# Packed value columns, a shared root and an early copy of the first head in the second attention of a two-layer block

## The reference

```python
h = rms_norm(x, norm_g)
mq, mk, mv, mg, dq, dk, dv, dg = split(h @ w_in)      # 8 standard heads of 64; 4 differential heads
# standard heads: causal softmax attention with a linear bias by distance
m_out = softmax(mq @ mk.T * scale - slope * dist) @ mv * silu(mg)
# differential heads: two softmaxes over one value of width 128, then a norm of its own
d_out = (softmax(q1 k1) - lam * softmax(q2 k2)) @ dv
d_out = rms_norm(d_out, subln) * 0.8 * silu(dg)
x = x + concatenate([m_out, d_out]) @ w_out
```

## Time and profile before

| | us |
|---|---|
| median of 3 runs | 1016.03 (1015.81 to 1016.11) |
| the profiled execution, its time | 1016.16 |
| its span | 1014.0 |
| TensorE busy | 1002.1 (99%) |
| VectorE busy | 557.6 (55%) |
| GpSimd busy | 502.3 (50%) |
| ScalarE busy | 454.1 (45%) |

### The profile page before, as it was taken

How to read it: one execution, slowest core, us unless ns; L and a number is a source line. 1 busy time by engine, 2 the same in 40 slices (tenths; PEclk the granted TensorE clock), 3 DMA queues, 4 the chain that set the end, 5 groups by cost and what they waited for, 6 DMA issues and landing times.

```text
span 1014.0 us, 13704 instructions
## 1 busy us (share of the span) xinstructions
PE 1002.1 (99%) x5051; PEld 835.4 (82%) x5051; DVE 557.6 (55%) x943; ACT 454.1 (45%) x682; POOL 502.3 (50%) x296
## 2 busy tenths in 40 slices
PE   9999999999999999999999999999999999999998
PEld 7888888888888988888888888889888778777787
DVE  6799897887633964334334310116715276676731
ACT  7222346898644532322322322233454347667630
POOL 4444365842346134444444465453387545755562
PEclk9999999999999999999999999999999999999999
DMA  7232222212244032332322323333132120111112
GB/s 258 83 104 93 95 83 67 80 63 84 73 176 151 17 102 86 103 101 85 103 100 87 103 104 104 104 123 106 43 104 83 63 84 22 64 63 43 42 63 83
DMA packets 26402, 91.11 MB, mean 90 GB/s; under 512 B 3056, under 2 KB 3184, under 8 KB 26224
## 3 DMA queue, kind: packets, MB, share of 16 engines
q1 hardware_dynamic: 26352, 90.42, 26.4%
HBM read 88.31 MB, written 2.10 MB: 89 GB/s over the span
## 4 chain that ended last, share of the span: by engine, by line
PE 89%; DVE 7%; ACT 2%; issue 1%; DMA 1%; POOL 0%; SPq 0%; DVEq 0%
PE ps L463 27%; PE ps L465 27%; PE ps L464 27%; PE ps L927 2%; PE ps L951 1%; DVE resid L2014 1%; PE ps L624 1%; PE ps L640 1%; DVE a_lo L1664 1%; DMA resid<-x_t 1%; DVE sq_x L1657 1%; DVE q_raw L1657 1%; DVE mix L1657 1%; DVE b_lo L1664 1%; PE ps L656 0%
## 5 line engine op out<-in xcount | busy, mean ns | idle before, releaser
L2362 POOL TENSOR_TENSOR w_lo<-w_raw,w_hi 128x1024 fp32r<-128x1024 f32 x137 | 325.8, 2379 | 410.6 <-ACT w_hi L1128 357.9
L1128 ACT ACTIVATE w_hi<-w_raw 128x1024 fp32r<-128x1024 f32 x133 | 139.2, 1047 | 279.6 <-PE ps L465 279.6
L463 PE MATMUL ps<-a_hi,w_hi 128*128 128x512 f32 (+1 forms) x544 | 211.6, 389 | 4.6 <-DVE v_lo L1661 3.1
L465 PE MATMUL ps<-a_hi,w_lo 128*128 128x512 f32 (+1 forms) x544 | 207.0, 380 | 0.0
L464 PE MATMUL ps<-a_lo,w_hi 128*128 128x512 f32 (+1 forms) x544 | 206.8, 380 | 0.0
L463 PE MATMUL ps<-b_hi,w_hi 128*128 128x512 f32 x392 | 152.9, 390 | 0.0
L465 PE MATMUL ps<-b_hi,w_lo 128*128 128x512 f32 x392 | 152.6, 389 | 0.0
L464 PE MATMUL ps<-b_lo,w_hi 128*128 128x512 f32 x392 | 152.5, 389 | 0.0
L463 PEld LDWEIGHTS ps<-a_hi,w_hi 128*128 128x128 f32 x544 | 102.3, 188 | 28.3 <-DVE v_lo L1661 4.4
L465 PEld LDWEIGHTS ps<-a_hi,w_lo 128*128 128x128 f32 x544 | 102.3, 188 | 20.0
L464 PEld LDWEIGHTS ps<-a_lo,w_hi 128*128 128x128 f32 x544 | 102.4, 188 | 18.3 <-issue 0.2
(11 more groups left out here) (339 smaller groups left out, 1727.1 us busy)
## 6 DMA issues: line engine op xcount, KB each, us to landing
w_raw<-weights SPq DMA_DIRECT2D x156, 512.0 KB, 3.2
resid<-x_t SPq DMA_DIRECT2D x8, 256.0 KB, 6.6
w_raw<-weights SPq DMA_DIRECT2D x8, 256.0 KB, 6.6
resid<-x_t SPq DMA_DIRECT2D x1, 2048.0 KB, 8.8
out_t<-out_sb SPq DMA_DIRECT2D x8, 256.0 KB, 2.0
vec<-vecs SPq DMA_DIRECT2D x1, 220.0 KB, 7.1
vec<-vecs SPq DMA_DIRECT2D x1, 4.0 KB, 1.6
```

Source lines behind the costliest of these rows:

```text
L463: pe.matmul(out, s_hi, m_hi, start=first, stop=False, skip_group_check=True)
L465: return pe.matmul(out, s_lo, m_hi, start=False, stop=last, skip_group_check=True)
L1128: act.activation(w_hi[:, k % 2, 0:width], w_raw[:, k, 0:width], ACT.Copy).then_inc(hi_ready, 1)
L2362: pool.tensor_tensor(w_lo[:, k % 2, 0:width], w_raw[:, k, 0:width], w_hi[:, k % 2, 0:width].bitcast(F32), ALU.subtract).then_inc(lo_ready, 1)
```

## The change

Values of standard heads are packed as four groups of 64 columns per key block: high of half 0, low of half 0, low of half 1, high of half 1 (`v2_parts`). One matmul of 128 columns gives a head's high-value product on 64 partitions and its low-value product on the other 64, so a head needs two matmuls per block, with `pt_hi` and with `pt_lo`. Each head now fills the whole bank by itself. So ScalarE copies the high half's rows out (`out_copy`), VectorE adds the other half's (`head_add`), and only then may the next head use the bank. The gate product of standard chunks moves to GpSimd, except the last. Of the Newton step two products move to GpSimd (`root_squares`), with the factor -0.5 moved into `variance` and undone in `first_root`. `root` comes after the scores' last part. Some of ScalarE's steps change order.

```diff
-        v2_hi = put("v2_hi", [P, TB, P + 64], F32R)
-        v2_lo = put("v2_lo", [P, TB, P + 64], F32R)
+        v2_parts = put("v2_parts", [P, TB, 4, 64], F32R)
...
@@ tensor: values2
                 if head == 0:
                     pe.wait_ge(v2_lo_ready, max(c + 1, 2))
                     if not is_diff(c):
-                        pe.wait_ge(gap_zeroed, 2)
                         pe.wait_ge(dvar_ready, c // 2 + 1)
                     elif c:
                         pe.wait_ge(out_read, c // 2)
+                else:
+                    pe.wait_ge(head_added, c // 2 + 1)
                 pe.wait_ge(ptl_ready, tq + 1)
+                part = 2 * half_of(c, head)
                 for j in range(TB):
...
+                    out = ps[:, OUT_BANK, j * P:T]
+                    if is_diff(c):
+                        mm = products(out, vd_hi[:, j, :], vd_lo[:, j, :], pt_hi[:, w], pt_lo[:, w], first=j == 0)
+                    else:
+                        values = v2_parts[:, j, part:part + 2, :].rearrange("p a f -> p (a f)")
+                        pe.matmul(out, values, pt_hi[:, w], start=j == 0, stop=False, skip_group_check=True)
+                        mm = pe.matmul(out, values, pt_lo[:, w], start=False, stop=j == TB - 1, skip_group_check=True)
                 mm.then_inc(av2_ready, 1)
...
@@ scalar
+            def out_copy(c, head):
+                rows = slice(64 * half_of(c, head), 64 * half_of(c, head) + 64)
+                act.wait_ge(av2_ready, tq_of(c, head) + 1)
+                if head == 0 and c > 1:
+                    act.wait_ge(mixed_ready, c - 1)
+                act.activation(att2[rows, 1, :], ps[rows, OUT_BANK, :], ACT.Copy).then_inc(head_copied, 1)
...
-                    act.wait_ge(out_read, c // 2 + 1)
+                    act.wait_ge(gated_ready, c // 2 + 1)
...
                 if c:
+                    out_copy(c - 1, 0)
                     high_probs(c - 1, 1)
                     exponentials(c, 2)
                     high_mixed(c - 2)
+                    stage_qk2(c + 1)
                     split_unit(v_unit(c + 2))
+                    out_copy(c - 1, 1)
                     split_unit(g_unit(c + 1))
                     stage_v2(c + 1)
                 high_probs(c)
+                exponentials(c + 1, 0)
                 if c:
                     high_mixed(c - 1)
-                exponentials(c + 1, 0)
-                if c:
                     split_unit(v_unit(c + 3))
...
-                stage_qk2(c + 3)
-
+
+            out_copy(KC - 3, 0)
             high_probs(KC - 3, 1)
             exponentials(KC - 2, 2)
+            high_mixed(KC - 4)
+            stage_qk2(KC - 1)
+            out_copy(KC - 3, 1)
             split_unit(g_unit(KC - 1))
             stage_v2(KC - 1)
...
             gate_sigmoid(KC - 1)
+            out_copy(KC - 1, 0)
             high_probs(KC - 1, 1)
...
             split_out(4)
+            out_copy(KC - 1, 1)
             high_mixed(KC - 1)
@@ vector
-            def gated(c):
+            def head_add(c, head):
...
+                high, small_ = 64 * half_of(c, head), 64 - 64 * half_of(c, head)
+                dve.wait_ge(head_copied, 2 * (c // 2) + head + 1)
+                tt(att2[high:high + 64, 1, :], att2[high:high + 64, 1, :], ps[small_:small_ + 64, OUT_BANK, :], ALU.add
+                   ).then_inc(out_read if head else head_added, 1)
...
             def root(c):
                 dve.wait_ge(drs_ready, c // 2 + 1)
-                V.do(tt(d_sq[:, :], d_y[:, :], d_y[:, :], ALU.mult))
+                dve.wait_ge(root_square, 2 * (c // 2) + 1)
                 V.do(dve.scalar_tensor_tensor(out=d_y[:, :], in0=att2[:, 0, :], scalar=small[:, 7:8], in1=d_y[:, :],
                                               op0=ALU.mult, op1=ALU.mult))
-                V.wait(back=1)
-                V.do(dve.scalar_tensor_tensor(out=d_sq[:, :], in0=d_sq[:, :], scalar=-0.5, in1=d_v[:, :],
-                                              op0=ALU.mult, op1=ALU.mult))
                 V.wait()
+                dve.wait_ge(root_square, 2 * (c // 2) + 2)
                 dve.scalar_tensor_tensor(out=att2[:, 0, :], in0=d_sq[:, :], scalar=1.5, in1=d_y[:, :],
                                          op0=ALU.add, op1=ALU.mult).then_inc(d_final, 1)
...
                 value_drain(c + 3)
+                biased(c + 2, 2)
                 root(c)
-                biased(c + 2, 2)
+                head_add(c + 1, 0)
                 low_probs(c + 1, 1)
                 joined(c + 2, (3, 2, 0, 1))
                 gate_row(c + 1)
+                head_add(c + 1, 1)
                 gate2_drain(c + 2)
                 slopes(c + 3)
                 value_low(c + 3)
-                if c + 2 < KC:
-                    gated(c + 1)
-            gated(KC - 1)
+            last_gated(KC - 1)
@@ gpsimd
+            def root_squares(c):
+                pool.wait_ge(drs_ready, c // 2 + 1)
+                pool.tensor_tensor(d_sq[:, :], d_y[:, :], d_y[:, :], ALU.mult).then_inc(root_square, 1)
+                pool.wait_ge(root_square, 2 * (c // 2) + 1)
+                pool.tensor_tensor(d_sq[:, :], d_sq[:, :], d_v[:, :], ALU.mult).then_inc(root_square, 1)
+            def gated(c):
...
+                pool.tensor_tensor(att2[:, 1, :], att2[:, 1, :], gate_e[:, chunk_of(c), :], ALU.mult).then_inc(gated_ready, 1)
...
-            pool.memset(v2_hi[:, :, 64:P].bitcast(F32), 0.0).then_inc(gap_zeroed, 1)
-            pool.memset(v2_lo[:, :, 64:P].bitcast(F32), 0.0).then_inc(gap_zeroed, 1)
...
                 gate_silu(c)
+                root_squares(c)
                 gated_out(c)
                 pool.wait_ge(p2_joined, c // 2 + 2)
                 stage_qk(c + 3)
                 if c + 4 < KC:
                     low_unit(v_unit(c + 4))
+                gated(c + 1)
                 low_unit(g_unit(c + 3))
                 mixed_low(c)
...
             gate_silu(KC - 2)
+            root_squares(KC - 2)
             low_out(1)
             gated_out(KC - 2)
             gate_silu(KC - 1)
```

More of the change, by code:

```diff
@@ L234, in two_layer_block @@
         sq_hi = (place("sq_hi0", [P, 4, T], F32R, at["pt_hi"] + 4 * T * KC), place("sq_hi1", [P, 4, T], F32R, at["b_hi"]))
-        assert at["sq_hi0"] + 4 * T * 4 <= at["vd_lo"] + 4 * T
+        assert at["sq_hi0"] + 4 * T * 4 <= limit
         gate_g = place("gate_g", [P, KC, T], F32, at["b_lo"])
@@ L297, in two_layer_block @@
             sem("drs_ready"), sem("d_final"), sem("att2_final"), sem("mixed_ready"))
-        pool_held, gap_zeroed = sem("pool_held"), sem("gap_zeroed")
+        pool_held, head_added, gated_ready = sem("pool_held"), sem("head_added"), sem("gated_ready")
+        head_copied, root_square = sem("head_copied"), sem("root_square")
         first_done, first_sq, first_acc, first_drained = (
@@ L955, in values2 @@
                 tq = tq_of(c, head)
-                at_col = 64 * half_of(c, head)
                 if c >= KC:
                     return
[L959 to L962, removed]
                 if head == 0:
@@ L969, in values2 @@
                         pe.wait_ge(out_read, c // 2)
+                else:
+                    pe.wait_ge(head_added, c // 2 + 1)
                 pe.wait_ge(ptl_ready, tq + 1)
+                part = 2 * half_of(c, head)
                 for j in range(TB):
[L972 to L975, removed]
+                    w = slice(P_COL[j], P_COL[j] + (TB - j) * P)
+                    out = ps[:, OUT_BANK, j * P:T]
[5 more added lines that the diff above has]
+                        mm = pe.matmul(out, values, pt_lo[:, w], start=False, stop=j == TB - 1, skip_group_check=True)
                 mm.then_inc(av2_ready, 1)
@@ L1496, in stage_v2 @@
                 else:
-                    act.activation(by_heads(v2_hi[:, :, :])[:, :, 0:3:2, :], by_heads(src), ACT.Copy).then_inc(v2_hi_ready, 1)
+                    act.activation(v2_parts[:, :, 0:4:3, :], by_heads(src), ACT.Copy).then_inc(v2_hi_ready, 1)
             def exponentials(c, part):
@@ L1539, in first_root @@
                 act.wait_ge(dvar_ready, c // 2 + 1)
-                A.do(act.activation(d_y[:, :], d_v[:, :], ACT.Ln))
+                A.do(act.activation(d_y[:, :], d_v[:, :], ACT.Ln, scale=-2.0))
                 A.wait()
                 act.activation(d_y[:, :], d_y[:, :], ACT.Exp, scale=-0.5).then_inc(drs_ready, 1)
+            def out_copy(c, head):
[4 more added lines that the diff above has]
+                act.activation(att2[rows, 1, :], ps[rows, OUT_BANK, :], ACT.Copy).then_inc(head_copied, 1)
             def high_mixed(c):
@@ L1617, in _ @@
                 exponentials(c + 2, 1)
-                stage_qk2(c + 3)
+            out_copy(KC - 3, 0)
             high_probs(KC - 3, 1)
             exponentials(KC - 2, 2)
+            high_mixed(KC - 4)
+            stage_qk2(KC - 1)
+            out_copy(KC - 3, 1)
             split_unit(g_unit(KC - 1))
             stage_v2(KC - 1)
```

(30 more changed lines are left out.)

## The result

| | before | after |
|---|---|---|
| median, us | 1015.99 (12 runs, eleven of them 1015.59 to 1016.36) | 1018.71 (12 runs, 1015.16 to 1019.00) |
| ratio, from all the runs and not from the two medians | | 1.0018, 95% interval 1.0010 to 1.0026 |
| profiled execution: time, span | 1016.16, 1014.0 | 1015.16, 1013.3 |
| instructions of TensorE | 5051 | 5019 |

One of the twelve runs before took 2005.39 us, for a cause that nothing here shows; it stays out of the ratio, and without it the median is 1015.98.

The account below looks back on a forecast made before the run. The prediction took TensorE to bound the kernel, busy 1002.1 of 1014.0 us. Its terms, -1.6 + 0.4 + 0.8, summed to -0.4 us, giving 1015.7 us, with a range of 1013.0 to 1018.3.

Parts of the forecast that it names:

- pair 1, pair 2: First two chunk pairs of the second attention: TensorE waits for GpSimd's w_lo but starts 0.8 us earlier in each.
- pair 3: Third chunk pair: GpSimd's added gate product delays the last gate unit's residue, so TensorE starts 0.4 us later than before.
- last pair: Root squares delay output weight 1's residue: TensorE starts 1.4 us later, less 0.62 for head 1, +0.8 us.
- What goes from TensorE: Values of the eight standard heads: a third of each head's matmuls goes, 0.62 us each, 5.0 us if nothing waits.
- Head 1's probabilities: VectorE's pt_lo starts only 0.16 us earlier because out_copy goes first; TensorE loses some 0.16 us, leaving 1.08 a pair.
- Root and head_add on VectorE: GpSimd's squares fit its idling before the root; VectorE ends in time for pt_lo, with about 0.2 us to spare.
- Rival D: The squares come late and hold head_add and pt_lo by 0.4 us in three pairs: 1016.9 us, chance 0.06.
- GpSimd behind k_lo, pairs 1 and 2: The slope row gets in between k_lo and w_lo; TensorE then waits for w_lo, starting 0.8 us earlier, twice.
- Rival C: Slower through the shared port: each contested handover goes against the engine TensorE needs, +2.9 us, 1018.9 us; chance 0.12.
- Rival A: GpSimd's insertions don't hold TensorE in pair 3 and at the end: -3.9 us, 1012.1 us; chance 0.15.

Follow-up runs that it names:

- w1_first: The changed kernel with the residue of output weight 1 back ahead of GpSimd's root squares of the last pair; median 1015.99 us, ratio 0.9999.
- before_wait2: The kernel before, with two unneeded GpSimd products ahead of the residue of the last gate unit; median 1018.43 us, ratio 1.0020.
- gated_behind: The changed kernel with GpSimd's gate product of the standard chunk behind the residue of the next gate unit; median 1014.38 us, ratio 0.9992.
- both_moved: The changed kernel with both GpSimd moves: output weight 1's residue ahead of the root squares, gate product behind the gate unit's residue; 1013.38 us, ratio 0.9978.
- after_again: The changed kernel unaltered, timed anew against the kernel before; median 1017.33 us, ratio 1.0019.

## Why the prediction was wrong

Times are taken from the last norm row that TensorE waits for (821.57 before, 821.10 after), since all that lies ahead of it does the same work in both kernels, and the row's start varies from 820.91 to 821.88 between the kept traces.

| term | predicted | measured in the execution at full clock |
|---|---|---|
| pair 1, pair 2 | -0.8, -0.8 | -0.71, -0.74 |
| pair 3 | +0.4 | +0.48 |
| last pair: wait for output weight 1, and head 1 | +1.4 - 0.62 | +1.42 - 0.60 |
| ahead of the stage | 0 | -0.47 |
| sum of the terms | -0.4 | -0.15, and -0.6 with the part ahead (0.1 more of the span is in no term) |
| clock | not in the sum | in all executions: +1.7 us for each fall, 31 falls in 46 chances |

- *What goes from TensorE*: right. 32 matmuls, 5.0 us.
- *Head 1's probabilities*: right in kind. Against pair 1, pt_lo starts 0.1 us earlier (0.16 predicted), since out_copy holds ScalarE for 0.62 us and not 0.47. TensorE's loss at head 1 is 0.3 us with the slower first interval (0.16 predicted).
- *Root and head_add on VectorE*: right. The squares lie in GpSimd's idling, pt_lo waits for pt_hi and not for the root. The squares of d_y took 1.04 us, less than my 1.28. Rival D did not come.
- *GpSimd behind k_lo, pairs 1 and 2*: right, the slope row's place too. Rival C did not come there; in the last pair one root product went ahead, as in the forecast.
- *Pair 3* and *the last pair*: the starts are right to 0.1 us, and so is the wait before output weight 1 (2 us, measured 1.95). The wait before the last gate unit is not. I wrote of 1.5 us. I had counted it from the start before, less the gain, and forgotten that this start itself ended a wait of 1.02 us. TensorE stood 2.50 us.
- The step that failed is the pricing of these two waits by their length alone ("it starts 0.4 us later than before", "+0.8"). A wait of 2.5 us let the clock fall in 16 of 22 executions of w1_first and before_wait2, one of 1.95 us in 4 of 11. (That the falls of gated_behind stand behind the wait of 1.95 us follows from their going with it, not from a trace.) This puts 1.7 us for each fall on top, with two falls in half of the changed kernel's executions, and carries 1015.5 to 1018.8. No rival had it; in the trace of before, TensorE once running waits nowhere longer than 1.03 us and the clock is full, so nothing in it tested a longer wait. Rival C, the slow side, gave 1018.9 for a wrong reason: that the median came near it is luck. Without the clock the forecast of 1015.7 was close: the full-clock executions take 1015.2 to 1015.8.
- *Rival A* ("don't hold TensorE"): both_moved is its test. It had 1012.1 and the kernel takes 1013.2, at full clock; the difference is the 0.84 us wait that came in place of the one removed and a third pair that gives 0.7, not 1.08.

## What to carry to other kernels

Where TensorE is busy nearly all the time, look for the longest single wait that a change makes, not for the sum of the waits: here a wait of 2.4 to 2.5 us cost its length and, in 16 of 22 executions, 1.1 to 1.5 us more, and even one of 1.95 us did so in 4 of 11, by 2.1 us. Count it from the end of TensorE's last work, not from where it started before. When work moves to an engine with idle time, what counts is whether the idling lies ahead of or behind the event that the next deadline hangs on; here the same instructions, one place further back in GpSimd's list, turned 1018.7 into 1013.3 us. And read the granted clock of every timed execution beside the one profile: this one, at full clock, showed a faster kernel than the median is.

## What the runs showed of the hardware that I had not expected

- The cost of a fall is nearly the same within a kernel and differs between kernels: the steps of the changed kernel lie at 1015.4, 1017.2 and 1018.8 us; by the means at each clock the step is 1.5 us in w1_first, 2.1 us in gated_behind and 1.1 us in before_wait2. In after_again the clock fell about 1 us behind the wait, in before_wait2 the first matmul behind it was slow.
- At a given wait the clock falls in some executions and not in others: 2.39 and 2.49 us, 16 of 22; 1.95 us, 4 of 11; 1.40 us or less, 1 of 50 (five kernels). What decides in a single execution stays open.
- A VectorE instruction that was held up during one GpSimd instruction was let in before the next one in every case read here, and GpSimd's next then took 0.1 to 0.4 us longer (1.47 and 2.81 us above, for 1.30 and 2.40). Even an instruction of four columns is held: 1.19 us for 0.22.
- A copy or an add on 64 partitions takes as long as on 128: 0.59 us (out_copy) against 0.58 us, 0.68 us for head_add.
